# Eight head pairs of a hybrid decoder step: three chunk steps a pair become two, and the samples are solved beside them

## The reference, cut to what matters

```python
def _wkv_step(S, inp):
    r, w, k, v, kk, kka = inp
    sa = jnp.einsum('bhij,bhj->bhi', S, -kk)
    S = S * w[:, :, None, :] + sa[..., None] * kka[:, :, None, :] + v[..., None] * k[:, :, None, :]
    y = jnp.einsum('bhij,bhj->bhi', S, r)
    return S, y
...
    mod = jax.nn.silu(c) @ lp['w_ada'] + lp['b_ada']
    sh1, sc1, g1, sh2, sc2, g2 = [m[:, None, :] for m in jnp.split(mod, 6, axis=-1)]
    h = x * (1 + sc1) + sh1
    proj = h @ lp['w_in']
```

## Time and profile before

| what | value |
|---|---|
| median of 3 runs | 4428.61 us (4426.52 to 4431.79) |
| profiled execution, first to last instruction | 4444.1 us |
| eight head pairs, from PE's first step 0 (500.5 us) to the last mean (1711.4 us) | about 1211 us |
| one pair in the middle, mean to mean | 157 us |
| PE busy over the span | 91% |

### The profile page before, as it was taken

The page is one execution under the profiler, slowest core; times in us unless marked ns, Lnnn a source line. Parts: engine busy times, 40 slices in busy tenths (PEclk is TensorE's granted clock), DMA queues, the critical chain, the costliest instruction groups (busy, mean ns, idle before and its releaser), DMA issues. The chain is left out here.

```text
span 4444.1 us, 72112 instructions
## 1 busy us (share of the span) xinstructions
PE 4041.6 (91%) x29289; PEld 3836.3 (86%) x29289; DVE 3034.1 (68%) x3965; ACT 1459.4 (33%) x2056; POOL 1473.1 (33%) x778
## 2 busy tenths in 40 slices
PE   5897899999899866989999999999997999999997
PEld 4897787888788755979999999999997999999996
DVE  1565453554455353246998888888877999999996
ACT  1343321221222111124233444444424444444333
POOL 0332322222232220002356444444433444444441
PEclk7998888988888876999999999999998999999998
DMA  8221222222222213212247999999998999999994
GB/s 365 82 88 51 79 76 77 95 76 73 88 85 65 77 65 143 86 57 99 82 145 255 379 384 374 380 386 386 385 358 328 373 377 387 373 378 380 377 356 172
DMA packets 214274, 982.33 MB, mean 221 GB/s; under 512 B 21953, under 2 KB 101953, under 8 KB 106561
## 3 DMA queue, kind: packets, MB, share of 16 engines
q1 hardware_dynamic: 92256, 524.19, 31.2%
q0 software_dynamic: 57984, 409.37, 23.4%
q10 hardware_dynamic: 63840, 46.15, 3.2%
HBM read 917.54 MB, written 62.09 MB: 220 GB/s over the span
## 5 line engine op out<-in xcount | busy, mean ns | idle before, releaser
L93 PE MATMUL PS<-first_HH,tail_WH 128*128 128x352 f32 (+1 forms) x3072 | 974.0, 317 | 59.6 <-DVE first_HL L1744 32.0
L95 PE MATMUL PS<-first_HH,tail_WL 128*128 128x352 f32 (+1 forms) x3072 | 958.4, 312 | 0.0
L94 PE MATMUL PS<-first_HL,tail_WH 128*128 128x352 f32 (+1 forms) x3072 | 956.3, 311 | 0.0
L93 PE MATMUL PS<-dn_BH,tail_WH 128*128 128x352 f32 x2048 | 669.1, 327 | 38.2 <-DVE dn_BL L2324 25.0
L95 PE MATMUL PS<-dn_BH,tail_WL 128*128 128x352 f32 x2048 | 660.2, 322 | 0.0
L94 PE MATMUL PS<-dn_BL,tail_WH 128*128 128x352 f32 x2048 | 658.6, 322 | 0.0
L93 PEld LDWEIGHTS PS<-first_HH,tail_WH 128*128 128x128 f32 x3072 | 582.3, 190 | 64.1 <-issue 32.0
L2300 POOL DMA_INDIRECT dn_VR<-in_v_rows,tail_EI x192 | 435.1, 2266 | 574.9 <-DVEq L2343 553.8
L2049 POOL DMA_INDIRECT up_UR<-in_u_rows,tail_EI x192 | 423.1, 2204 | 501.0 <-DVEq L2130 481.1
L94 PEld LDWEIGHTS PS<-first_HL,tail_WH 128*128 128x128 f32 x3072 | 583.3, 190 | 0.5
L95 PEld LDWEIGHTS PS<-first_HH,tail_WL 128*128 128x128 f32 x3072 | 581.9, 189 | 0.0
(11 more groups left out here) (401 smaller groups left out, 7854.4 us busy)
## 6 DMA issues: line engine op xcount, KB each, us to landing
tail_WR<-in_peer_u SPq DMA_DIRECT2D x128, 1024.0 KB, 9.0
tail_WR<-in_peer_v SPq DMA_DIRECT2D x128, 1024.0 KB, 8.1
mix_RING<-in_w_ada SPq DMA_DIRECT2D x88, 1024.0 KB, 4.9
mix_RING<-in_w_in SPq DMA_DIRECT2D x37, 1024.0 KB, 4.9
tmp_z<-up_ZB ACTq DMA_DIRECT2D x128, 176.0 KB, 7.7
tmp_gd<-up_STG ACTq DMA_DIRECT2D x22, 1024.0 KB, 18.4
dn_GG<-tmp_gd SPq DMA_DIRECT2D x16, 1408.0 KB, 10.1
dn_ZI<-tmp_z SPq DMA_DIRECT2D x128, 176.0 KB, 6.1
```

What stands on the lines that cost most here:

```text
L93: nc.tensor.matmul(out, r32(wh), r32(xh), start=first, stop=False)
L94: nc.tensor.matmul(out, r32(wh), r32(xl), start=False, stop=False)
L95: return nc.tensor.matmul(out, r32(wl), r32(xh), start=False, stop=last)
```

## The change

Each pair runs two steps instead of three. The samples are packed as 32 columns (8 x 4, tile SL). In step 0 PE makes their transposes and key products (`smp_turn`), a start value from the states (`smp_rows`), three hops of substitution (`smp_solve`, each followed by DVE's `smp_hop_add`) and the outputs (`smp_out`); POOL spreads the result (UX) and scales the states (SI); two products of 512 columns (`pe_tail`) and two DVE additions make the new states. The state updates of step 1 (`pe_scan(pe, i, 1, n)`) go between parts of `project(i + 2, 0)`, which now stands whole ahead of the mean; `project(i + 2, 1)` stands in halves before and behind the variance, and only `which` 2 stays behind the head sum. The modulation goes four and four, one tile right behind the key products of each step and one behind L1035, and is turned and read inside the same step. `low(i + 2, 2)` on POOL now stands behind the landing of both state outputs.

```diff
-    LEVELS = (5, 5, 2)
+    MODS = (4, 4)
+    LEVELS = (5, 5)
...
-        def project(pe, i, which, part=(0, 1)):
...
-                for kt in range(KT):
+                for kt in range(*kts):
...
         def pe_scan(pe, i, step, n):
 
+            bank = (7, 3)[step]
             pe.wait_ge(s_ready, 18 * i + 9 * step + n + 1)
+            nc.tensor.matmul(PS[:, bank, CH_CHUNK * n:CH_CHUNK * n + CH_CHUNK], SB[:, n, :],
...
+        def pe_modulation(pe, i, t):
+
+            if t == 4:
+                pe.wait_ge(mod_read, 2 * i + 1)
+            pe.wait_ge(ada_in, 16 * ADA_PAIR * i + 16 * (t + 1))
+            for k in range(KT):
...
+        def smp_turn(pe):
+
+            nc.tensor.transpose(PS[0:64, 7, 0:P], SL[:, KBH:KKH + 1, :].rearrange("p k t -> p (k t)"), IDENT[:])
...
+            for h in range(2):
+                rows = slice(64 * h, 64 * h + 64)
+                mm = nc.tensor.matmul(PS[0:64, 6 + h, 2 * P:2 * P + 64],
...
+        def smp_rows(pe, i):
+
+            pe.wait_ge(si_in, 32 * i + 32)
+            pe.wait_ge(smp_masked, i + 1)
+            pe.wait_ge(smp_kept, i + 1)
+            for n in range(NB):
+                nc.tensor.matmul(PS[0:NT4, 7, 3 * P:4 * P], AD[:, NT4 * n:NT4 * n + NT4], SI[:, n, :],
...
+            for h in range(2):
+                mm = nc.tensor.matmul(PS[0:NT4, 7, 3 * P + 64 * h:3 * P + 64 * h + 64], MS[NT4:2 * NT4, h, 0, :],
...
+            mm.then_inc(smp_x, 1)
...
+        def smp_solve(pe, i, hop):
...
+            for h in range(2):
+                mm = nc.tensor.matmul(PS[0:NT4, 7, P * (hop % 2) + 64 * h:P * (hop % 2) + 64 * h + 64],
+                                      MS[0:NT4, h, 0, :], (UU if hop else X0)[0:NT4, 64 * h:64 * h + 64],
...
+            mm.then_inc(smp_hop, 1)
...
+        def smp_out(pe, i):
+
+            pe.wait_ge(smp_hopped, HOPS * i + HOPS)
+            for n in range(NB):
+                nc.tensor.matmul(PS[:, 7, 2 * P + NS * n:2 * P + NS * n + NS], SI[:, n, :],
...
+            for h in range(2):
+                mm = nc.tensor.matmul(PS[64 * h:64 * h + 64, 7, 2 * P + NT4:2 * P + 2 * NT4],
...
+            mm.then_inc(smp_y, 1)
...
             if step:
-                pe_turn(pe, i, step - 1)
-                if step == 1:
-                    pe_modulation(pe, i, 3)
                 pe.wait_ge(gk_read, u)
+            else:
+                smp_turn(pe)
...
+            if step == 0:
+                pe.wait_ge(smp_masked, i + 1)
+            pe_modulation(pe, i, 4 * step)
...
             if step:
                 pe.wait_ge(gk_ready, u)
+                pe.wait_ge(smp_yt, i + 1)
+            else:
+                smp_rows(pe, i)
...
                 if step:
-                    pe_scan(pe, i, step - 1, 2 * lv - 2)
-                if step == 2:
-
-                    pe_modulation(pe, i, 6, 0, 5)
-                    pe_scan(pe, i, 1, 1)
-                    pe_modulation(pe, i, 6, 5, 10)
-                    pe_scan(pe, i, 1, 2)
-                    pe_modulation(pe, i, 6, 10)
-                elif lv == 3 or (lv == 1 and step == 0):
-                    pe_modulation(pe, i, 3 * step + lv // 2)
+                    pe_scan(pe, i, 0, 2 * lv - 2)
+                if lv in (1, 3):
+                    pe_modulation(pe, i, 4 * step + 1 + lv // 2)
...
                 if step:
-                    pe_scan(pe, i, step - 1, 3 if step == 2 else 2 * lv - 1)
-            if step < 2:
-                pe_modulation(pe, i, 3 * step + 2)
+                    pe_scan(pe, i, 0, 2 * lv - 1)
+                elif lv <= HOPS:
+                    smp_solve(pe, i, lv - 1)
...
+            pe_modulation(pe, i, 4 * step + 3)
...
-            if step == 2:
-
-                for n in range(4):
-                    pe_modulation(pe, i, 7, 4 * n, 4 * n + 4)
-                    pe_scan(pe, i, 1, 4 + n)
+            if step == 0:
+                smp_out(pe, i)
...
-                if step == 2 and x == 0:
-                    pe_turn(pe, i, 2)
+                if x == 0:
+                    pe_turn(pe, i, step)
...
+
+            u = 2 * i + 1
+            pe.wait_ge(smp_spread, i + 1)
+            pe.wait_ge(y0_ready, 2 * u + 2)
+            for half in range(2):
+                mm = nc.tensor.matmul(PS[:, 4 + half, :], TS[0:64, :], UX[0:64, 4 * half:4 * half + 4, :],
+                                      start=True, stop=True)
+            mm.then_inc(smp_state, 1)
+            units = [(half, kt) for half in range(2) for kt in range(KT)]
             if ahead2:
-                pe.wait_ge(mod_read, 3 * i + 3)
-                project(pe, i + 2, 0, (0,))
+                pe.wait_ge(mod_read, 2 * i + 2)
+                for half, kt in units[:8]:
+                    project(pe, i + 2, 0, (half,), (kt, kt + 1))
             pe.wait_ge(gk_ready, u + 1)
-            pe.wait_ge(y0_ready, 2 * u + 2)
-            pe.wait_ge(si_in, 32 * i + 32)
             for n in range(8):
...
+                pe_scan(pe, i, 1, n)
+                if ahead2:
+                    for half, kt in units[8 + 3 * n:11 + 3 * n]:
+                        project(pe, i + 2, 0, (half,), (kt, kt + 1))
+
+        def pe_mean(pe, i):
+
+            pe.wait_ge(yt_ready, 2 * i + 2)
...
-            if ahead2:
-                project(pe, i + 2, 0, (1,))
+
+        def pe_variance(pe, i):
...
+            project(pe, 1, 1)
+
             def pair(i, ahead, ahead2):
-                if ahead:
-                    project(pe, i + 1, 1)
                 pe.wait_ge(banks_idle, i + 1)
...
-                for step in range(3):
+                for step in range(2):
                     pe_step(pe, i, step)
-                pe_samples(pe, i, ahead2)
-                pe_post(pe, i, ahead2)
+                pe_tail(pe, i, ahead2)
+                pe_mean(pe, i)
+                if ahead2:
+                    project(pe, i + 2, 1, (0,))
+                pe_variance(pe, i)
+                if ahead2:
+                    project(pe, i + 2, 1, (1,))
...
+            if step == 0:
+                act.wait_ge(smp_masked, i + 1)
+                A(TS[0:64, :], PS[0:64, 7, 0:P], ACT.Copy)
+                A(UU[NT4:2 * NT4, :], PS[NT4:2 * NT4, 7, P:2 * P], ACT.Copy)
+                act.drain().then_inc(smp_kept, 1)
...
+            if step == 0:
+                act.wait_ge(smp_x, i + 1)
+                A(X0[0:NT4, :], PS[0:NT4, 7, 3 * P:4 * P], ACT.Copy).then_inc(smp_x_kept, 1)
...
-                    if ahead2 and step == 0:
-                        low(pool, i + 2, 0)
-                    if step == 2:
-                        pool.wait_ge(sp_ready, i + 1)
-                        for h in range(2):
-                            rows = slice(64 * h, 64 * h + 64)
-                            pool.dma_start(io["wkv_p"][i][rows], SB[rows, 8, rows]).then_inc(sp_out, 16)
-                        pool.wait_ge(sp_out, 32 * i + 32)
-                        pool.sem_inc(sp_free, 1)
+                    if step == 0:
+                        pool.wait_ge(smp_kept, i + 1)
+                        pool.wait_ge(smp_hopped, HOPS * i + HOPS)
+                        G.tensor_tensor(UX[0:64], bcast(UU[0:64, :], 1, NB), bcast(SMK[0:64, 1, NS - 1:NT4:NS], 2, P),
+                                        ALU.mult)
+                        pool.drain().then_inc(smp_spread, 1)
+                        if ahead2:
+                            low(pool, i + 2, 0)
+                pool.wait_ge(smp_y, i + 1)
+                for h in range(2):
+                    rows = slice(64 * h, 64 * h + 64)
+                    G.tensor_tensor(SI[rows, :, rows], SI[rows, :, rows], bcast(PI[rows, PC0 + NS:PC1:NS + 1], 2, 64),
+                                    ALU.mult)
+                pool.drain().then_inc(smp_scaled, 1)
                 if ahead2:
                     low(pool, i + 2, 1)
                 pool.wait_ge(so_ready, i + 1)
                 for h in range(2):
                     rows = slice(64 * h, 64 * h + 64)
-                    pool.dma_start(io["wkv_s"][i][rows], K0[rows, :, rows]).then_inc(so_out, 16)
+                    pool.dma_start(io["wkv_s"][i][rows], SI[rows, :, rows]).then_inc(so_out, 16)
+                pool.wait_ge(sp_ready, i + 1)
+                for h in range(2):
+                    rows = slice(64 * h, 64 * h + 64)
+                    pool.dma_start(io["wkv_p"][i][rows], SB[rows, 8, rows]).then_inc(sp_out, 16)
+                pool.wait_ge(so_out, 32 * i + 32)
                 if ahead:
                     load_states(i + 1)
+                pool.wait_ge(sp_out, 32 * i + 32)
+                pool.sem_inc(sp_free, 1)
                 if ahead2:
                     low(pool, i + 2, 2)
-                pool.wait_ge(so_out, 32 * i + 32)
-                pool.sem_inc(so_free, 1)
                 pool.wait_ge(post_done, i + 1)
                 pool.dma_start(io["mix"][i], YT[:]).then_inc(y_out, 16)
...
+        def smp_hop_add(dve, i, hop):
+
```

(43 more changed lines are left out.)

177 lines of the change are left out of this document (85 added, 92 removed).

## The result

The changed kernel takes 4255.6 us (median of 4 runs, 4247.7 to 4270.8) beside 4430.2 us of the kernel before (4426.5 to 4435.1): a ratio of 0.960 with a 95% interval of 0.9577 to 0.9623, 167 to 187 us less. The forecast was 4228 us with a range of 4196 to 4282.

A forecast was written before the change was run, and what follows sets the result against it. PE's executed work and its clock were taken as the bound. Middle pairs at -25.5 us, with pairs 0, 6 and 7 at -21.2, -27.9 and -23.6, gave -200: a 4244 us span, 4228 us median, range 4196 to 4282.

The forecast's parts named there:

- The sum: All terms of a middle pair together: -26.9 + 5.7 + 0 - 4.3 = -25.5 us, so 131 us a pair.
- Ahead of the steps: Stretch before step 0: half a projection leaves, DVE becomes the bound; -4.3 us, to about 35.9, bounds 35.0 and 40.2.
- the three pieces: Ahead of the steps: head-sum wait 0.70, about 1.0 of 1.6 before step 0, and 2.6 of a collision with POOL go.
- The rival that DVE keeps its stretch: Ahead of the steps: POOL's split hits another DVE row, stretch stays at 40.2 us; 4254 us in all, chance 0.14.
- Step 0: First step of a pair: 8.1 us of added PE work against filled waits, +5.7 us, bounds +3.5 and +12.
- The rival with the sample chain on the path: Step 0 at +9.5 instead of +5.7 us, from open hops and copies or held DVE rows; 4258 us, chance 0.08.
- Step 1: Second step: earlier key products offset an extra modulation tile and the turn; 0 us, bounds -2 and +2.
- The tail: After step 1: 46.24 us go, state products, projection and eight updates take 19.3; -26.9 us, bounds 18.5 and 24.5.
- the return of 0.2: In the tail: extra cost of the first projection product behind other work, eight times, 1.6 us.
- the clock as a rival: Head of step 0 and whole tail at 1.2 GHz, +6 and up to +6 us a pair; 4270 to 4320, chance 0.09.
- a clock of 0.9 or more in the tail: Sign of being right: PE's granted clock in the tail, with an update every 1.6 to 1.9 us.
- The rival that the updates do not hide: In the tail: eight updates cost 1.10 us each instead of 0.45, +31 us in all; 4259 us, chance 0.07.

The follow-up runs named there:

- b2_var_early: Against the changed kernel, the second projection stands whole again at the head of the next pair, behind the variance: 4273 us, ratio 0.9638.
- the last run: Changed kernel with projection units at step 1's end, plus step 0's turn of modulation tiles moved behind step 1's transposes: 4218.3 us, ratio 0.9505.

## Why the prediction was right

**The sum** of the terms came out at -24.1 us a pair for a forecast of -25.5, and each term near its own. Part of the gain is clock, which the terms hold without naming it: a middle pair of before had 40 us at 1.2 GHz, one of after 22.5 (2 x (1 - c) of each window). The tail's 6.8 us at that clock cost it 3.1, so the 18 us that went are worth some 8 of the 24, an estimate from that one price.

**Ahead of the steps** (-4.7 for -4.3). DVE became the bound, as worked out; PE waits 2.6 us for it. But the three pieces did not come as forecast, and that their sum did is partly luck. The multiplication beside POOL's split went from 4.64 to 1.43 us, -3.2 for -2.6; DVE's last row now ends 0.18 us ahead of step 0 in place of 1.6, -1.4 for -1.0; and the 0.70 ahead of the head sum's row, which was to go, stands as before:

```profile
743.16 0.73 DVE L1378 TENSOR_SCALAR rw_SUMS<-PS 128x552 f32<-128x552 f32 x1 [0.70 <-issue]
759.15 0.18 DVE L1415 TENSOR_TENSOR rw_BO<-rw_CHN,PS 128x32 f32<-128x32 f32 x1
```

The bare collision with POOL's split showed in b2_var_early: 3.5 us of the stretch. The rival that DVE keeps its stretch is out.

**Step 0** (+5.9 for +5.7). Its two halves came as forecast: in the third pair PE's busy time rose by 36.70 - 29.13 = 7.6 us for the 8.1 of new rows, and its idle time fell from 3.2 to 0.7, as the 2.4 of filled waits had it. Leaving out rows costed at 3.4 us took 2.5 away. The rival with the sample chain on the path (+9.5) is out.

**Step 1** (-0.4 for 0). 1.0 of the 2.03 us stayed as the wait for `gk_read`, as I had said it would not be saved whole; the last run took that too.

**The tail** (-24.8 for -26.9) is the term that was mis-sized, by two errors of opposite sign. I had 19.3 us at 2.4 GHz. There it measures 18.0, below my lower bound of 18.5: the state products take 1.9 for my 1.55, but the return of 0.2 that I added to each update is already inside the 0.45 (and without the returns my own sum gives 17.7, not 18.5). And the first 7 to 8 us of it run at 1.2 GHz, which costs 3.1 to 3.7. I had the clock as a rival with a chance of 0.09, and a clock of 0.9 or more in the tail as a sign of being right; it was 0.82 to 0.84 in nearly every one of pairs 0 to 5. It came in part only, in the tail's first third and not at the head of step 0. What I took as evidence against it was evidence for it: the window of 0.85 is 2 x 0.15 x 11.75 = 3.5 us at 1.2 GHz, and in the kernel before, the first projection products of that window already stand 0.23 apart:

```profile
919.86 0.43 PE L94 MATMUL PS<-mix_HLT,mix_RINGR 128*128 128x276 f32 x1
920.09 0.43 PE L95 MATMUL PS<-mix_HHT,mix_RINGR 128*128 128x276 f32 x1
```

The rival that the updates do not hide is out: no update in the tail waits for DVE, and undoing that part costs 62 us by the windows (8 + 2.3, six times).

**From span to median** is where most of the miss lies: 4255.6 is 27 us above the forecast. 9 of them are the sum, 200 for the 191 that the eight pairs lost in the first two profiles (188 on the mean of two profiles of before and three of after), and 2 are before's own median, 4430.2 for 4428.6. The other 16 lie between profiled executions and medians, and no trace shows where, as only the profiled executions have one: that of before was long, and that of after was the shortest of its four. I took the 15.5 us between the profiled span and the median as constant. The profiled execution of the changed kernel was 4246.1 us long by its span and 4247.7 by its time, so the two differ by 1.6 only, as in every later run; the 15.5 were the scatter of one long execution. That the first spans differ by 198 us, so near to my 200, is luck: 7 of them lie outside the pairs. Seven pairs, in three profiles of after and two of before, differ by (1089.8 - 923.8) / 7 = 23.7 us each.

## What to carry to other kernels

A round trip between two engines is worth moving into dense work of the one that is busy (here about 10 of a pair's 24 us), and what it costs there is read as a pitch, neighbours included; an addition for the return would count it twice. Where a forecast moves dense rows behind short ones, it needs a term for the clock, priced from the same rows at both levels. And a difference between two executions of the same kernel is to be taken for scatter until a second profile shows that it isn't.

## What was not expected of the hardware

PE's clock fell to 1.2 GHz while PE was busy without a wait, in the turn and the chunk matrices at the end of a step or in the state products behind them, and stayed there into the tail's dense products (0.82 over its window, 1.00 in the stretch behind it). A busy PE is not by that at 2.4 GHz: step 2 of before had it busy for 31.67 of 34.49 us, at 0.70. Sixteen more products at the end of step 0 went with 0.96 in step 0 and 0.78 in the tail in one pair, and with 0.84 and 1.00 in another; which rows decide it stays open.

A DVE scan beside a POOL subtraction of 128 x 2048 took 5.52 us in place of 1.31, a reciprocal beside such a one 3.56, for 3.55 without it; the multiplication of the earlier trace rows had 4.64 and 0.72.
